# The last stage's gather of two 4 KB vectors per pick: one transfer into one ring, or two transfers into two rings

## The reference

```python
q = (xt @ wq).reshape(P_BLOCK, P_HEADS, 2, P_HALF)
s = jnp.einsum('nhpd,hpkd->nhpk', q, keys)
s1, i1 = lax.top_k(s[:, :, 0], P_TOPK)
s2, i2 = lax.top_k(s[:, :, 1], P_TOPK)
...
top_s, pos = lax.top_k(cand_s, P_TOPK)
idx = jnp.take_along_axis(cand_i, pos, axis=-1).reshape(P_BLOCK, P_HEADS * P_TOPK)
g = jax.nn.softmax(top_s.astype(jnp.float32), axis=-1).reshape(P_BLOCK, P_HEADS * P_TOPK).astype(xt.dtype)
act = jax.nn.gelu(jnp.einsum('nd,ned->ne', xt, u[idx]), approximate=False)
return jnp.einsum('ne,ned->nd', g * act, v[idx])
```

## Time and profile before

| | |
|---|---|
| median of 3 runs | 3922.02 us (3916.95 to 3926.28) |
| profiled execution, its own time | 3920.97 us |
| span of its instructions | 3919.2 us |
| mean granted clock of TensorE | 0.945 of full speed |
| busy: PE, DVE, ACT, POOL | 86%, 49%, 18%, 25% of the span |
| read from DRAM | 1128.96 MB |

### The profile page before, as it was taken

One profiled execution on the slowest core, in us unless ns is written; L12 is line 12 of the kernel. 1 busy time (PEld: TensorE's weight loads), 2 busy tenths in 40 slices (PEclk: granted clock), 3 DMA queues, 4 the chain that ended last, 5 costly groups with the idle time before them and its releaser, 6 DMA issues. The chain is left out here.

```text
span 3919.2 us, 37507 instructions
## 1 busy us (share of the span) xinstructions
PE 3376.9 (86%) x11902; PEld 1491.6 (38%) x11903; DVE 1928.6 (49%) x3951; ACT 688.9 (18%) x1609; POOL 964.2 (25%) x829
## 2 busy tenths in 40 slices
PE   7997999788889987999887987898878888788887
PEld 3345454422223322333224456544333333333332
DVE  5834323622333322333225226486666766766776
ACT  1011121000000000000002125422222222222212
POOL 1000000112221222012122013134443444444443
PEclk8998999789999999999998998999998999999998
DMA  9834434469999999197976201179999999999998
GB/s 330 285 124 166 152 122 157 187 240 411 370 375 353 363 407 374 62 380 270 397 290 242 81 6 44 44 291 378 421 421 399 417 417 412 421 404 421 415 422 341
DMA packets 194149, 1157.36 MB, mean 295 GB/s; under 512 B 25659, under 2 KB 27995, under 8 KB 74356
## 3 DMA queue, kind: packets, MB, share of 16 engines
q1 hardware_dynamic: 97140, 565.17, 37.3%
q0 software_dynamic: 80576, 564.05, 35.2%
q10 hardware_dynamic: 16320, 26.75, 2.2%
HBM read 1128.96 MB, written 48.68 MB: 300 GB/s over the span
## 5 line engine op out<-in xcount | busy, mean ns | idle before, releaser
L1170 PE MATMUL ps<-wt,e_xT 128*64 128x512 f32 x3200 | 743.4, 609 | 114.2 <-DMA wt<-in_w_exp 113.0
L2628 DVE SCALAR_TENSOR_TENSOR mod<-uv,mix 128x1024 f32<-128x1024 f32 x512 | 626.9, 1225 | 352.4 <-DMA uv<-in_peer_uv,q_picks 347.7
L2312 POOL DMA_INDIRECT uv<-in_peer_uv,q_picks x512 | 575.4, 1124 | 773.4 <-PE ps L2403 702.7
L2403 PE MATMUL ps<-uv,q_dg 128*128 128x512 f32 x1024 | 519.9, 664 | 134.4 <-ACT q_dg L2480 129.9
L2403 PE MATMUL ps<-uv,tri 128*128 128x512 f32 x1024 | 472.2, 615 | 75.9 <-ACT tri L2480 75.9
L1150 POOL COPY wt<-e_land 128x2048 f32<-128x2048 f32 x124 | 248.0, 2030 | 1004.3 <-PE ps L1170 951.8
L1170 PEld LDWEIGHTS ps<-wt,e_xT 128*64 128x64 f32 x3200 | 219.7, 139 | 596.2 <-issue 380.8
L2403 PEld LDWEIGHTS ps<-uv,q_dg 128*128 128x128 f32 x1024 | 213.7, 214 | 431.7 <-issue 431.7
L1170 PE MATMUL ps<-wt,e_aT 128*64 128x512 f32 x1600 | 354.2, 595 | 2.8 <-ACT e_aT L1223 2.8
L2403 PEld LDWEIGHTS ps<-uv,tri 128*128 128x128 f32 x1024 | 197.8, 197 | 345.6 <-issue 345.6
L472 PE MATMUL ps<-hT,wt 128*128 128x512 f32 x640 | 285.1, 602 | 1.5 <-DVE wt L799 1.5
(11 more groups left out here) (458 smaller groups left out, 3508.3 us busy)
## 6 DMA issues: line engine op xcount, KB each, us to landing
wt<-in_w_exp SPq DMA_DIRECT2D x260, 1024.0 KB, 20.0
e_land<-in_w_exp SPq DMA_DIRECT2D x124, 1024.0 KB, 24.2
wt<-in_w_in_units SPq DMA_DIRECT2D x15, 2048.0 KB, 11.2
mod<-in_w_mod_units SPq DMA_DIRECT2D x48, 512.0 KB
scratch_xs<-const_zeros SPq DMA_DIRECT2D x8, 2080.0 KB
mod<-in_w_ada_units SPq DMA_DIRECT2D x32, 512.0 KB
p_ring<-in_w_in SPq DMA_DIRECT2D x7, 2048.0 KB, 10.6
e_xg<-scratch_xs ACTq DMA_DIRECT2D x104, 128.0 KB
```

The source lines that it names most:

```text
L1170: ins = nc.tensor.matmul(ps[64 * h:64 * h + 64, at, :], lhs[:, k % 4, 64 * (k // 4):64 * (k // 4) + 64], wt[:, u, a, h * W:(h + 1) * W], s ...
L2312: pool.indirect_dma_start(out=uv[:, slot(n), :, :].rearrange("p a d -> p (a d)"), out_offset=None, in_=A["peer_uv"], in_offset=bass.Indire ...
L2403: last = nc.tensor.matmul(acc(t)[:, c, :], dg(n), uv[:, slot(n), 1, c * W:(c + 1) * W], start=fresh, stop=closing)
L2628: dve.scalar_tensor_tensor(junk[:, n % 2, :], uv[:, slot(n), 0, :], 1.0, mix[:, tile_of(k), :], ALU.mult, ALU.mult, accum_out=ap[:, k % 2, ...
```

## The change

Each pick gets two indirect DMAs in place of one: 128 rows of 4 KB from `u`, then 128 rows of 4 KB from `v`, straight from the two tables. The same 20 rows of SBUF (80 KB per partition) are now two rings: 8 rows for `u` and 12 for `v`. A row of the `u` ring is free when the dot of pick `n - 8` is done (`s_u`), and a row of the `v` ring when the matmuls of pick `n - 12` are done (`s_v`). Each row has a semaphore of its own for landing. Dots wait for `u` alone, matmuls for `v` alone. The joined table is gone.

```diff
+        UROWS = (8, 9, 10, 11, 12, 13, 0, 1)
+        VROWS = (14, 15, 16, 17, 18, 19, 2, 3, 4, 5, 6, 7)
+        NU, NV = len(UROWS), len(VROWS)
...
-        s_uv = [sem(f"uv{i}") for i in range(NR)]
+        s_us, s_vs = [sem(f"us{i}") for i in range(len(UROWS))], [sem(f"vs{i}") for i in range(len(VROWS))]
...
-                    if n == KEYS:
+                    if n == KEYS - 1:
                         pool.wait_ge(s_kt, 1)
...
-                    if n >= NR:
-                        pool.wait_ge(s_v, n - NR + 1)
-                    pool.indirect_dma_start(out=uv[:, slot(n), :, :].rearrange("p a d -> p (a d)"), out_offset=None,
-                                            in_=A["peer_uv"],
-                                            in_offset=bass.IndirectOffsetOnAxis(ap=picks[:, n:n + 1], axis=0)
-                                            ).then_inc(s_uv[n % NR], 16)
+                    at = bass.IndirectOffsetOnAxis(ap=picks[:, n:n + 1], axis=0)
+                    if n >= NU:
+                        pool.wait_ge(s_u, n - NU + 1)
+                    pool.indirect_dma_start(out=urow(n), out_offset=None, in_=A["peer_u_2"], in_offset=at).then_inc(s_us[n % NU], 16)
+                    if n >= NV:
+                        pool.wait_ge(s_v, n - NV + 1)
+                    pool.indirect_dma_start(out=vrow(n), out_offset=None, in_=A["peer_v_2"], in_offset=at).then_inc(s_vs[n % NV], 16)
...
-                    pe.wait_ge(s_uv[n % NR], 16 * (n // NR + 1))
+                    pe.wait_ge(s_vs[n % NV], 16 * (n // NV + 1))
...
-                    dve.wait_ge(s_uv[n % NR], 16 * (n // NR + 1))
+                    dve.wait_ge(s_us[n % NU], 16 * (n // NU + 1))
```

More of the change, by code:

```diff
@@ L2246, in groups, with urow, vrow @@
             return [(G * g, G) for g in range(BATCH // G - 1)] + [(BATCH - G + g, 1) for g in range(G)]
-        def slot(n):
-            return (n + SHIFT) % NR
+        def urow(n):
+            return uv[:, UROWS[n % NU] // 2, UROWS[n % NU] % 2, :]
+        def vrow(n):
+            return uv[:, VROWS[n % NV] // 2, VROWS[n % NV] % 2, :]
         def dg(n):
@@ L2399, in _ @@
                     closing = j == BATCH - 1 and (h == PH - 1 or t >= 2)
-                    pe.wait_ge(s_uv[n % NR], 16 * (n // NR + 1))
+                    pe.wait_ge(s_vs[n % NV], 16 * (n // NV + 1))
                     pe.wait_ge(s_dg, n + 1)
                     for c in range(2):
-                        last = nc.tensor.matmul(acc(t)[:, c, :], dg(n), uv[:, slot(n), 1, c * W:(c + 1) * W],
+                        last = nc.tensor.matmul(acc(t)[:, c, :], dg(n), vrow(n)[:, c * W:(c + 1) * W],
                                                 start=fresh, stop=closing)
@@ L2627, in dot @@
                         dve.wait_ge(s_w, (k - 1) * (BATCH // G))
-                    dve.scalar_tensor_tensor(junk[:, n % 2, :], uv[:, slot(n), 0, :], 1.0, mix[:, tile_of(k), :],
+                    dve.scalar_tensor_tensor(junk[:, n % 2, :], urow(n), 1.0, mix[:, tile_of(k), :],
                                              ALU.mult, ALU.mult, accum_out=ap[:, k % 2, j:j + 1]).then_inc(s_u, 1)
@@ L2781 @@
 SCRATCH = dict(xs=[(NBLK + 2) * BLK, D], modr=[24, W], o=[3, T, OW], line=[3, AH, LINE], lines=[P, 3, AH, LINE])
-FLAT = {"x": (T, D), "ctx_2": (TC, D), "peer_uv": (NK * NK, 2 * D)}
+FLAT = {"x": (T, D), "ctx_2": (TC, D), "peer_u_2": (NK * NK, D), "peer_v_2": (NK * NK, D)}
 def kernel(**inputs):
@@ L2790 @@
     arrays, A, K = {}, {}, {}
-    inputs["peer_uv"] = np.concatenate([np.asarray(inputs.pop("peer_u_2")), np.asarray(inputs.pop("peer_v_2"))], -1)
     gate, up, down = (np.asarray(inputs.pop(n)).reshape(NE, 4, 2, P, D) for n in ("w_gate", "w_up", "w_down"))
```

## The result

| kernel | us, median | executions, range | before, same place | ratio, 95% interval |
|---|---|---|---|---|
| changed | 4076.16 | 4, 4074.82 to 4085.58 | 3922.28 | 1.0398, 1.0378 to 1.0419 |
| changed, on a second chip | 3952.38 | 4, 3945.07 to 3956.89 | 3922.26 | 1.0080, 1.0064 to 1.0097 |
| changed, on a third chip | 3947.50 | 4, 3944.75 to 3949.71 | 3920.86 | 1.0073, 1.0056 to 1.0090 |

The change made the kernel 154 us slower where it was first measured. I had predicted 3959 us and a range up to 4035, so the direction was right and the size far off. The two lower rows come from the end of the study. The same program, unaltered, costs 27 to 30 us on two other chips, while the kernel before takes the same time everywhere. So I read the 154 us as two parts: some 28 us that come with the change where nothing else happens, and some 125 us more that come with it in some places only.

The account below looks back on a forecast made before the run. From 2640 us full DMA engines bound the kernel. With POOL nearly as slow, 2.65 us a pick over 486 picks gives 1288 us against 1250, +38, end -1: 3958, as median 3959 us; range of 8 in 10, 3918 to 4035.

Parts of the forecast that it names:

- Rows' price: 4 KB rows for 8 KB in the last stage's DMA queue: factor 1.021, 25 us, bounds 12 to 72 us.
- Lists and dots: On POOL, a list starting inside a DVE dot waits for its end; two lists just fit between dots 2.54 us apart.
- mean over 1.1 us: Sign in the changed profile: POOL's mean list over 1.1 us means the dots' locks on lists stay.
- The rings: Deeper rings cover 1.5 to 2 picks more, 4 to 5 us, at each `queries` piece; nothing deducted of 24 us holes.
- Fixed time: Rival: each small transfer's fixed time shows when the gather queue runs low, over 1000 us more; chance 0.02.
- The sum: Last stage at 2.65 us a pick, 486 picks: 1288 us against 1250, +38; end -1; total 3959 us.
- regime of 2.76 us: Last stage with empty queues: dots hold each next `u` list, POOL sets the pace, DMA engines idle 8%.
- POOL keeps pace: Rival: in the last stage only the rows' price and the holes count, 3921 to 3946 us; chance 0.25.
- DVE, ACT and PE have the same work: Step for the 2640 to 3890 us stretch: these engines' work is unchanged, DVE busy 869 us, PE 1047; no cost added.
- POOL alone bounds: Rival: POOL's lists set the pace all the way, 2.76 or 2.85 us a pick, about 4012 or 4056 us; chance 0.18.
- DMA share under 0.98: Sign in steady 100 us windows of the changed profile: a share this low shows POOL's pace, not the rows' price.
- theories A and B: From the first experiments: A, lists and two-input dots collide; B, doubled landings or lists slow the signals.

Follow-up runs that it names:

- kernel with one-input dots: Changed kernel with each dot replaced by a plain sum over the row of `u`, no multiplication with tokens: 3940.74 us, on another chip 3943.18 us.
- the pair in the old ring: Kernel before with two 4 KB-row transfers per pick in its ring of ten, one matmul wait ahead of both: 3960.46 us, on another chip 3971.66 us.
- the tiny list: Kernel before plus a second indirect transfer of 16-byte rows per pick, read by nobody: 3964.10 us, on other chips 3967.34 and 3961.80 us.
- the small transfers by SP: Kernel before plus a small transfer issued by SP after each of 448 dots, doubling landings but not POOL's lists: 3933.64 us, 1.0041.

## Why the prediction was right or wrong

**Rows' price: right in kind, a little small.** I took a factor of 1.021, 25 us. The undisturbed 100 us show 409 GB/s against 421, 1.029, so 2.56 us a pick and 35 us over the 1204 us of the stretch. That lies inside my bounds of 12 to 72. The DMA engines set the 409, not POOL. The kernel with one-input dots has the same 409 while its POOL waits 107 us in all for free rows. That kernel takes 21 us more than before on its chip, but this is the price less what the rings give back, and not the price alone.

**Lists and dots: right in kind, too dear in size.** Two lists of 0.94 to 1.02 and their 0.30 do fit between two dots. The means are 999 and 1019 ns, not the 1124 of before, so "mean over 1.1 us" failed. One input in place of two saves 3952.38 - 3943.18 = 9 us, though the sum takes as long as the dot (1219 ns, 1225 before). That is a two-input dot's part with the new rings.

**The rings: they give back part of the holes.** I had deducted nothing for them. On one chip the new rings take 3952.38 us where the pair in the old ring takes 3971.66, 19 us less, with 12 and 19 us between the executions of each. The stretch has 405 GB/s against 398. The window at the first `queries`, at 358 GB/s before, is at 410, but with the pair in the old ring it is at 409, so this window doesn't show the rings' part.

**Fixed time: absent.** Transfers that land 13.0 us after their issue leave no gap between them. The fit of the Trainium skill (DMA: Bandwidth & Descriptors, section "Anatomy of one DMA — SWDGE (gpsimd) path"), by which I had estimated 6.4 us a pair, doesn't bear on a queue that is kept full. Here a pair takes 2.63 us.

**The sum, where there are no stalls: near, and in part by luck.** 2.63 us a pick against 2.65, +27 to +30 us against +38. But my 2.65 was the middle between full queues and a regime of 2.76 us in which the DMA engines idle 8% and POOL sets the pace. That regime never came. The share is 1.02 over the whole stretch, though POOL has no slack either: 953 us of lists, 270 of steps between them and 27 of waits are its 1250 us. What happened is my rival "POOL keeps pace". With 35 us for the rows in place of 25, its 3921 to 3946 us become 3931 to 3956, and the two places gave 3947.50 and 3952.38.

**The step that failed** is "DVE, ACT and PE have the same work", costed at nothing. They have the same work in every place. But the step rests on waits that end as quickly as before, and where the result was taken they don't: DVE waited up to 5.1 us for its own last instruction. A pick took 2.92 us there in place of 2.63, and the engines' own work is the same. Why these waits end late stays open. The term is (4076.16 - 3922.28) - 30 = 124 us, and it had no place in the sum and no rival. My rival "POOL alone bounds" has times nearby (4012 to 4056), but a different cause. The DMA share under 0.98, which I had named as the sign of POOL's pace, is here a sign of the stalls.

**What brings the stalls.** Shown: a place of one kind (three against three, if the first chip is none of the later ones), and a pair of lists per pick in it, since the kernel before and its version with a second wait stay at 3921 there. Without effect on it: split or joined rings, places of rows, number, kind and order of waits. Not shown: whether doubled landings alone do it, whether it takes the 4 KB rows, and whether one-input dots are spared. The kernels for that ran only in places without stalls (the one-input dots and the tiny list beside the changed kernel itself, the small transfers by SP only beside the other three), so the misses that they gave theories A and B count for those places alone. Nor is it shown what differs between the places. The places differ in chip and in hour, and I can't part these two.

One candidate is left, and only argued. Landing marks come at 640 per 100 us before and at 1248 with pairs. Stalls hit several engines at once, and records go missing in the same stretches, a few also in the kernel before. That would fit a recorder that can't put its records away and holds up whoever makes one. The Trainium skill (NOTIFIC — the notification-queue block, section "7.1 Overflow: three behaviours, one of which stalls the engine") says that the block's internal pipeline always holds back its producers rather than lose a record. Its section "10. Constraints, capacities, measured rates" gives at least 6.6 million records a second as sustained, a ceiling not reached. Here the landing marks of the pairs alone are 12.5 million a second (1248 in 100 us). Against it, records are in fact lost here, and the places without stalls take the same rate with all 30173 landing records kept. Nothing was run with the recorder off. If it is so, the 124 us belong to the measurement and not to the kernel. Every execution of this study has its span and clock recorded, so none decides it.

## What to carry to other kernels

Splitting a full queue's 1 MB gathers in two cost 0.7 to 0.8% where nothing else happened, since a dearer byte (3%, 35 us) was paid back only in part by deeper rings. Count it in bytes and list time per pick, not in fixed times. When a trace shows waits without a real releaser on several engines at once, don't look for them in the program; run the unaltered kernel in another place first. And never compare an experiment with a number from another chip, however steady the kernel before is: the medians of mine stayed within 5 us in all places and told nothing of this. Its trace did, by a few missing records.

## What the runs showed of the hardware

- Two levels by place for one program: 4076.16, 3952.38 and 3947.50 us, with the kernel before at 3922.28, 3922.26 and 3920.86.
- In the places with stalls DVE waits up to 5.1 us for its own last result, and POOL, PE and DVE stall together.
- 4 KB rows in a full queue: 409 GB/s, 8 KB rows: 421.
- In the places with stalls landing records are missing even before the changed stage: 13540 to 13584 up to 2550 us, against 13597 in each trace of the others.
- A second wait on GpSimd, ahead of one that ends no sooner, costs nothing that can be measured (1.0006).
